# The scale of a norm moved behind the product: H turned unscaled within the mixer's last tiles, 1/rms multiplied in at each up tile

## The reference

```python
for layer in range(DEPTH_2):
    h = _rmsnorm_2(x, norm_mix[layer])
    ...
    x = x + y
    h = _rmsnorm_2(x, norm_ffn[layer])
    x = x + _conv_ffn(h, ffn_w_up[layer], ffn_conv_w[layer], ffn_conv_b[layer], ffn_w_down[layer])

def _conv_ffn(h, w_up, conv_w, conv_b, w_down):
    S = h.shape[1]
    u = h @ w_up                      # 1024 -> 2 * 2816
    u_pad = jnp.pad(u, ((0, 0), (FFN_CONV - 1, 0), (0, 0)))
    y = conv_b.astype(u.dtype)
    for j in range(FFN_CONV):         # 3 taps along the tokens
        y = y + u_pad[:, j:j + S, :] * conv_w[j]
    gate, up = jnp.split(y, 2, axis=-1)
    return (jax.nn.silu(gate) * up) @ w_down
```

## Time and profile before

| | |
|---|---|
| median of 3 executions | 1595.07 us (1594.04 to 1595.58) |
| the profiled execution | 1594.28 us |
| its span, first to last instruction | 1592.6 us |
| mean granted TensorE clock | 0.944 of full speed |
| busy share PE, PEld, DVE, ACT | 90%, 76%, 52%, 43% |
| first mixer's last addition to H starts | 1075.24 us |
| second mixer's last addition to H starts | 1392.68 us |
| last addition of the second feed forward starts | 1587.86 us |

### The profile page before, as it was taken

The page is one execution under the profiler, slowest core; times in us unless marked ns, Lnnn a source line. Parts: engine busy times, 40 slices in busy tenths (PEclk is TensorE's granted clock), DMA queues, the critical chain, the costliest instruction groups (busy, mean ns, idle before and its releaser), DMA issues.

```text
span 1592.6 us, 27418 instructions
## 1 busy us (share of the span) xinstructions
PE 1437.8 (90%) x11661; PEld 1214.2 (76%) x11661; DVE 830.7 (52%) x1471; ACT 683.9 (43%) x1184; POOL 10.6 (1%) x10
## 2 busy tenths in 40 slices
PE   7999999999899777877777779999999998999998
PEld 6999899899865344334443679988999895899997
DVE  6775453565512111112112569667777776567775
ACT  6443544543522111111111685455555564465553
POOL 1000000000000000000000100000000000000000
PEclk9999999999989998898987999989999996999999
DMA  6454354577999999999999444233655541336553
GB/s 232 159 159 155 110 165 130 167 270 276 358 402 419 420 419 417 420 421 419 421 420 415 154 134 139 83 115 102 204 189 186 175 136 53 99 114 212 172 180 125
DMA packets 173711, 372.03 MB, mean 234 GB/s; under 512 B 6912, under 2 KB 141184, under 8 KB 149008
## 3 DMA queue, kind: packets, MB, share of 16 engines
q1 hardware_dynamic: 173584, 370.21, 63.0%
HBM read 369.14 MB, written 1.05 MB: 232 GB/s over the span
## 4 chain that ended last, share of the span: by engine, by line
PE 65%; DMA 22%; DVE 6%; ACT 5%; issue 1%; SPq 1%; DVEq 0%; ACTq 0%
PE bank L581 17%; PE bank L582 16%; PE bank L583 16%; DMA wu<-in_expert_w_up_dram 14%; DMA wu<-in_expert_w_down_dram 5%; PE bank L1625 3%; PE bank L737 3%; DMA raw<-in_hgrn_w_in_dram 2%; DVE lo L545 2%; PE bank L1597 2%; ACT hi L534 1%; PE bank L1663 1%; PE bank L871 1%; DMA raw<-in_w_in_dram 1%; PE bank L846 1%
## 5 line engine op out<-in xcount | busy, mean ns | idle before, releaser
L545 DVE TENSOR_TENSOR lo<-raw,hi 128x1024 fp32r<-128x1024 f32 (+2 forms) x315 | 371.9, 1215 | 214.3 <-ACT hi L534 213.4
L581 PE MATMUL bank<-XH,hi 128*128 128x256 f32 x1416 | 406.8, 287 | 4.3 <-DVE lo L545 2.2
L582 PE MATMUL bank<-XL,hi 128*128 128x256 f32 x1416 | 401.8, 284 | 0.0
L583 PE MATMUL bank<-XH,lo 128*128 128x256 f32 x1416 | 401.5, 284 | 0.0
L534 ACT ACTIVATE hi<-raw 128x1024 fp32r<-128x1024 f32 (+2 forms) x315 | 317.2, 1047 | 74.5 <-PE bank L583 18.3
L581 PEld LDWEIGHTS bank<-XH,hi 128*128 128x128 f32 x1416 | 272.9, 193 | 12.3 <-issue 6.6
L582 PEld LDWEIGHTS bank<-XL,hi 128*128 128x128 f32 x1416 | 272.6, 193 | 0.8
L583 PEld LDWEIGHTS bank<-XH,lo 128*128 128x128 f32 x1416 | 272.4, 192 | 0.0
L1625 PE MATMUL bank<-wu,xg 128*32 128x256 f32 x2048 | 172.7, 439 | 52.0 <-DMA wu<-in_expert_w_up_dram 48.1
L1625 PEld LDWEIGHTS bank<-wu,xg 128*32 128x32 f32 x2048 | 71.8, 122 | 128.2 <-DMA wu<-in_expert_w_up_dram 66.3
L1663 PE MATMUL bank<-wu,hidT 128*32 128x256 f32 x1024 | 75.6, 412 | 35.4 <-DMA wu<-in_expert_w_down_dram 29.9
(11 more groups left out here) (347 smaller groups left out, 2203.2 us busy)
## 6 DMA issues: line engine op xcount, KB each, us to landing
wu<-in_expert_w_gate_dram SPq DMA_DIRECT2D x64, 1024.0 KB, 27.1
wu<-in_expert_w_up_dram SPq DMA_DIRECT2D x64, 1024.0 KB, 26.8
wu<-in_expert_w_down_dram SPq DMA_DIRECT2D x64, 1024.0 KB, 27.3
raw<-in_w_in_dram SPq DMA_DIRECT2D x44, 1024.0 KB, 5.2
raw<-in_ffn_w_up_dram SPq DMA_DIRECT2D x44, 1024.0 KB, 5.2
raw<-in_ffn_w_down_dram SPq DMA_DIRECT2D x22, 1024.0 KB, 5.0
raw<-in_hgrn_w_in_dram SPq DMA_DIRECT2D x16, 1024.0 KB, 5.4
raw<-in_w_branch_ret_dram SPq DMA_DIRECT2D x8, 1024.0 KB, 6.9
```

What stands on the lines that cost most here:

```text
L545: dve.tensor_tensor(lo_of(u), v, hi_of(u), ALU.subtract).then_inc(*WL.inc(u))
L581: pe.matmul(dst, first[0], first[1], start=start, stop=False)
L582: pe.matmul(dst, second[0], second[1], start=False, stop=False)
L583: return pe.matmul(dst, third[0], third[1], start=False, stop=stop)
```

## The change

- H is turned unscaled. `pe_turns` is a side of the mixer's last four tiles: after the first token half of tiles 1, 2 and 3 TensorE turns quarter 0, 1 and 2 of H (`pe_piece`, 4 transposes, into banks 4 to 6). ScalarE and VectorE make XH and XL of it with the gain alone (`act_piece`, `dve_piece`), and the squares of each quarter (`act_piece_squares`, `dve_piece_squares`).
- The first gate tile (`first`) goes to two banks, one a unit: K steps 0 to 5 of unit 0, the turn of quarter 3, K steps 0 to 5 of unit 1, the row of 1/rms (`pe_rows`: two matmuls of ones with a diagonal of 1/rms, so that each partition has the row), then K steps 6 and 7 of both units.
- VectorE copies the row to `rsb` and multiplies each up or gate tile by it, from the bank to `us` in SBUF (`scaled`); all taps read `us`. The bank is free after that multiplication.
- The splits in the feed forward are placed anew. ScalarE: up to u + 7 before the g taps, u + 8 between taps and silu, u + 9 before the up taps. VectorE: up to u + 6 before the g multiplication, u + 7 behind it, u + 8 before the up multiplication, u + 9 behind it, ahead of the taps. None stands behind DL but after the last group. The sides take one step a tile, not two.
- The Sqrt table is loaded in the mixer's first output tile, not behind its last.

```diff
     m = Room(region, tr_at)
-    xsF = m.new([P, 2, D], F32)
...
+    us, rsb, diag = [m.new([P, 2, T], F32) for _ in range(2)], m.new([P, T], F32), m.new([P, 2, P], F32)
+    sq_a, sq_d = m.new([P, 4, 256], F32), m.new([P, 4, 256], F32)
...
+        def pe_piece(i, p, made):
...
+            pe.wait_ge(*made.got("H", p))
+            for j in range(2):
+                for t in range(2):
+                    k = 2 * p + j
+                    done = pe.transpose(b.ap[:, j * T + t * P:j * T + t * P + P], H[:, t, k * P:(k + 1) * P], ident)
...
+        def pe_turns(i, made):
+
+            yield
+            for p in range(3):
+                yield
+                pe_piece(i, p, made)
+                yield
+
+        def pe_rows(i):
...
+            for t in range(2):
+                pe.wait_ge(*NORM.dve.got(i, "diag", t))
+                done = pe.matmul(b.ap[:, t * P:(t + 1) * P], C("ones"), diag[:, t, :], start=True, stop=True)
...
+        def dve_scale(i):
+            dve.wait_ge(*NORM.act.got(i, "sq", 3))
+            dve.wait_ge(*NORM.dve.got(i, "sq", 3))
+            dve.tensor_reduce(st[:, 48:50], st[:, 40:48].rearrange("p (t n) -> p t n", t=2), AX.X, ALU.add).then_inc(*NORM.dve.inc(i, "sums"))
+            dve.wait_ge(*NORM.act.got(i, "root"))
+            dve.reciprocal(st[:, 52:54], st[:, 50:52]).then_inc(*NORM.dve.inc(i, "rstd"))
+            dve.wait_ge(*NORM.dve.got(i, "rstd"))
+            for t in range(2):
+                dve.tensor_scalar(diag[:, t, :], ident, st[:, 52 + t:53 + t], None, ALU.mult).then_inc(*NORM.dve.inc(i, "diag", t))
...
+        def act_result(n, unit, made, w0):
+            for i in range(4):
+                act_wide(unit(i), AHEAD)
+                if i == 0:
+                    act_warm(ACT.Sqrt)
+                else:
+                    act_piece_squares(n, i - 1, made)
+                    act_piece(n, i - 1, "norm_ffn_2", w0)
+            act_piece_squares(n, 3, made)
+            act_root(n)
+            act_piece(n, 3, "norm_ffn_2", w0)
+
+        def dve_result(n, unit, made, w0):
+            for i in range(4):
+                dve_wide(unit(i), AHEAD)
+                if i:
+                    dve_piece(n, i - 1, "norm_ffn_2", w0)
+                dve.wait_ge(*WU.got(unit(i) + 1))
+                hs = H[:, :, 256 * i:256 * i + 256]
+                dve.tensor_tensor(hs, hs, b_[i].rearrange("p (t n) -> p t n", t=2), ALU.add).then_inc(*made.inc("H", i))
+                dve_piece_squares(n, i, made)
+            dve_scale(n)
+            dve_piece(n, 3, "norm_ffn_2", w0)
+            dve_rows(n)
...
+                for part in (range(6), range(6, 8)):
+                    for j in range(2):
...
+                        if k == 7:
+                            done.then_inc(*WU.inc(u + j))
+                        elif j == 0:
+                            pe_piece(4 + 2 * l, 3, made)
+                        else:
+                            pe_rows(4 + 2 * l)
...
+                dve.tensor_tensor(us[name == "u"][:, :, :], b_[(2 * j + (name == "u")) % 4].rearrange("p (h n) -> p h n", h=2),
+                                  rsb[:, :].rearrange("p (h n) -> p h n", h=1).to_broadcast([P, 2, T]), ALU.mult).then_inc(*F.dve.inc("us", name, j))
...
             for j in range(FT // 2):
                 r = j % 2
-                dve_tile(unit2(ffn_tile(l, "g", j)), 2, AHEAD, sides)
+                u = unit2(ffn_tile(l, "g", j))
+                dve_split(u + 7)
+                step(*sides)
+                scaled("g", j)
+                dve_split(u + 8)
                 other_taps("g", j, Y[0][r], 2 * j)
-                dve_tile(unit2(ffn_tile(l, "u", j)), 2, AHEAD, sides)
+                dve_split(u + 9)
+                step(*sides)
+                scaled("u", j)
+                dve_split(u + 10)
                 other_taps("u", j, Y[1][r], FT + 2 * j)
...
-                if j:
-                    dve_split(unit2(ffn_tile(l, "d", j - 1)) + 2 + AHEAD)
```

More of the change, by code:

```diff
@@ new lines, in pe_turns @@
+        def pe_turns(i, made):
[5 more added lines that the diff above has]
+        def pe_rows(i):
+            b = bank[4]
+            for s, key in b.taken:
+                pe.wait_ge(*s.got(*key))
+            for t in range(2):
+                pe.wait_ge(*NORM.dve.got(i, "diag", t))
+                done = pe.matmul(b.ap[:, t * P:(t + 1) * P], C("ones"), diag[:, t, :], start=True, stop=True)
+            done.then_inc(*NORM.pe.inc(i, "rows"))
+            b.taken = [(NORM.dve, (i, "rsb"))]
@@ new lines, in act_root, with dve_piece_squares @@
+        def act_root(i):
+            act.wait_ge(*NORM.dve.got(i, "sums"))
+            act.activation(st[:, 50:52], st[:, 48:50], ACT.Sqrt, bias=epst[:, 0:1], scale=1.0 / D).then_inc(*NORM.act.inc(i, "root"))
+        def dve_piece_squares(i, p, made):
+            dve.wait_ge(*made.got("H", p))
+            dve.scalar_tensor_tensor(sq_d[:, p, :], H[:, 1, 256 * p:256 * p + 256], 1.0, H[:, 1, 256 * p:256 * p + 256], ALU.mult,
+                                     ALU.mult, accum_out=st[:, 44 + p:45 + p]).then_inc(*NORM.dve.inc(i, "sq", p))
@@ L2123, in act_hgrn @@
                 step(*sides)
-            for i in range(4):
-                act_wide(unit2(16 + i), AHEAD)
-            act_warm(ACT.Sqrt)
+            act_result(4, lambda i: unit2(16 + i), HG.dve, 0)
         def dve_hgrn():
@@ L2184, in ffn_tile, with pe_ffn, first @@
             return t + n
-        def pe_ffn(l, sides):
+        def pe_ffn(l, made):
             F, x = FF[l], normed(4 + 2 * l)
-            pe_norm(4 + 2 * l, xsF)
+            def first():
+                u = unit2(ffn_tile(l, "g", 0))
+                for b in (bank[0], bank[2]):
+                    for s, key in b.taken:
+                        pe.wait_ge(*s.got(*key))
+                    b.taken = [(F.dve, ("us", "g", 0))]
+                for part in (range(6), range(6, 8)):
+                    for j in range(2):
+                        pe.wait_ge(*WH.got(u + j))
+                        pe.wait_ge(*WL.got(u + j))
+                        for k in part:
+                            for s, key in x(k):
+                                pe.wait_ge(*s.got(*key))
+                            done = three(b_[2 * j][:, 0:T], hi_of(u + j)[:, k, :], lo_of(u + j)[:, k, :], XH[:, k, :], XL[:, k, :],
+                                         False, k == 0, k == 7)
+                        if k == 7:
[4 more added lines that the diff above has]
+                            pe_rows(4 + 2 * l)
             def down(j, final):
@@ L2541, in act_mla @@
                     attend(h - 4)
-            for i in range(4):
-                act_wide(unit2(O_TILE + i), AHEAD)
-            act_warm(ACT.Sqrt)
+            act_result(6, lambda i: unit2(O_TILE + i), ML.dve, 8)
         def dve_mla(after):
@@ L2682, in dve_mla @@
                     attend(h - 4)
-            for i in range(4):
-                dve_wide(unit2(O_TILE + i), AHEAD)
-                dve.wait_ge(*WU.got(unit2(O_TILE + i) + 1))
-                hs = H[:, :, 256 * i:256 * i + 256]
-                dve.tensor_tensor(hs, hs, b_[i].rearrange("p (t n) -> p t n", t=2), ALU.add).then_inc(*X.dve.inc("H", i))
+            dve_result(6, lambda i: unit2(O_TILE + i), ML.dve, 8)
         rest_ = {}
```

96 lines of the change are left out of this document (63 added, 33 removed).

## The result

The changed kernel took 1581.03 us (median of 4 runs, 1577.41 to 1583.74), the kernel before, timed beside it, 1594.55 us (4 runs, 1592.74 to 1595.58): ratio 0.9915, 95% interval 0.9888 to 0.9942, a gain of 13.5 us. The profiled execution took 1583.74 us, span 1582.4.

A forecast was written before the change was run, and what follows sets the result against it. TensorE bounds the feed forward, with the norm ahead of it a hole. Terms -11.2 - 1.0 + 1.3 + 0.9 = -10.0 us gave a median of 1585.0 us, range 1581.0 to 1591.5.

The forecast's parts named there:

- going between kinds of matmul: At the two edges, TensorE changing kind of matmul ten times in all, 0.08 us each: 0.8 us of cost.
- lateness at the end of the first feed forward: Lateness of the group's chain not made good before the first feed forward's last down tile: +0.9 us.
- Part 1: Two edges: H's last addition to the first gate tile's end falls from 13.7 to 6.4 us; sum -11.2 us.
- Part 2: First feed forward: the weight-split wait at group 2's up tile goes, -1.0 us.
- Part 3: Every up or gate tile: 22 multiplications of 0.69 us per feed forward, covered as busy time; taps counted as unchanged.
- Part 4: Last down tile of each feed forward: DL late by 0.8 us in the first, 0.5 in the second; +1.3 us.
- Part 5: Group chain: starts some 5 us late, recovers 0.55 to 0.95 us a group, leaves +0.9 us in the first feed forward.
- the deepest case of the sum: Whole kernel: the largest gain claimed for any case, -13.5 us.
- A: Rival at the edges: they close only partly, XL or the diagonal late; gain 4 to 8 us, about 1589; chance 0.12.
- D: Rival at the edges: norm not shortened, the mixer's last tiles grow by what the edge loses; chance 0.01.
- C: Rival: no lateness at the end, nothing for changing kinds; -12 to -13.5 us, about 1582; chance 0.07.
- B: Rival in the feed forwards: chain longer than TensorE's group; no change (1594.5) to +6.6 us (1601.7); chance 0.14.

The follow-up runs named there:

- the shorter end: Changed kernel with the multiplication in halves, each with its own wait, and the last group's split moved behind DL: 1580.5 us (0.9919), again 1582.94 us (0.9947).

## Why the prediction was right or wrong

I predicted 1585.0 us, a gain of 10.0; by its stages the change is worth 11.4, and the first timing gave 13.5, outside the 8 to 12 that I called the forecast. Its 1581.03 us lie at the very bottom of my range. The mechanism was right, the sum too small. What failed is the size of two terms: the 0.8 us for going between kinds of matmul, which measured about nothing, and the 0.9 us of lateness at the end of the first feed forward, which measured nothing.

*Part 1, the edges: right, but for one term.* The first tile's end at 6.4 behind the last addition: TensorE starts its next tile at 6.37 and 6.43, busy all the way, at full clock. Two slips cancel in this: TensorE starts the tile 0.2 us ahead of the addition, and the rows of 1/rms (L732) are four records, not two, 0.43 us instead of 0.32. The 12 transposes at 1.3: 1.35 and 1.24. Cover of XL and of the diagonal: no wait on either. The 13.7 was 0.2 too long, since it ended with ScalarE's start and the 6.4 with TensorE's tile. Measured alike, the two edges save 7.09 + 7.06 = 14.15 and the tiles and the stage between give back 2.65, so 11.5, where I had 12.0. **The term that failed is the 0.8 for going between kinds of matmul**: the transposes run doubled and single leave between nothing and 0.07 us for six changes. I had taken it from a slow transpose of the earlier trace rows, which stands behind a hole, at lowered clock, and so could not price this.

*Part 2, the order of the splits: the size right, the weight wrong.* The wait of 1.1 went, as priced. But I treated this as a small item beside the multiplication. It is what the multiplication rests on: with the old order, the changed kernel is 56 us slower, and the new order alone changes nothing that can be measured. "As busy time it costs nothing: the matmuls cover it" was true only because of part 2, and nothing in my working said so. I summed VectorE's busy time of a group and never walked the two engines through their written order with the multiplication in it and the splits left where they were.

*Part 3, the multiplication:* 21 at 688 ns a feed forward and two halves, as priced. The taps from SBUF: VectorE's 480 ns against 477 from the bank, ScalarE's two 1.09 to 1.10 against 1.02. By the Trainium skill's VectorE: DVE Perf Modes (The TRN2 errata) the taps of one tile, two on ScalarE and four on VectorE, would have become, by an estimate, some 0.2 us shorter, which the rows do not show: of its two directions ScalarE's agrees with the rows and VectorE's does not.

*Part 4, the ends:* 0.8 and 0.5 forecast, 0.8 and 0.5 in the waits, both on DL. The attribution held too: the run without multiplications kept the 0.8 and lost the 0.5.

*Part 5, lateness: wrong by its whole 0.9.* Recovery was as worked out or a little better: from group 4 on late groups take 16.0 to 16.1 us of chain (I had 16.0 to 16.4) against 16.98, so nearly 1 us a group. What I had too large was the start. Counted back from DL of the last group in steps of 16.99, DL was 4.1 us late in group 1, where I had 5.2. The angles added the 2.5 that I had: DL came 18.01, 16.22 and 16.54 us after the one before in groups 2 to 4, against 16.37, 16.00 and 15.84 in the second feed forward, which has no angles. That makes 6.6 in all, not 7.7, and a part was made good meanwhile, so that the most was 5.1, in group 2. The lateness was gone by group 8, with the wait at the end the same 0.8 that the kernel before shows with the new order alone.

Summed: edges -11.5 (forecast -12.0), kinds of matmul 0 (+0.8), order -1.1 (-1.0), ends +1.3 (+1.3), lateness 0 (+0.9), unexplained -0.1: -11.4 (-10.0). That the unexplained is so small is in part luck: it is -0.2 in FF 0 and +0.1 in FF 1. Without the two allowances for things that no row showed, 1.7 together, the forecast would have been -11.7. Each was taken from within a bound whose lower end was zero, and in both zero was right, or nearly. The further 2.1 us of the first timing are not in the stages that the change touches, and the two later timings did not show them.

The range had a fault of its own: its lower end, 1581.0, was 0.6 us below the deepest case of the sum (1595.07 - 13.5 = 1581.6), with next to nothing for the scatter of a median. The kernel before alone had medians from 1592.5 to 1595.1 us, and three timings of the change gave 9.4, 13.5 and 11.6 us.

Of the rivals, A and D did not occur. C was right in its reasons (no lateness, nothing for changing kinds) and too deep in its sum. B did not occur here, but it is real: half a microsecond more of chain (multiplication twice at the up tile) already leaves lateness that costs 6.5 us, and with the old order the chain is longer than TensorE's group, 18.58 us.

## What to carry to other kernels

A norm's scale can be applied behind the product, and then only the matmul operands stand ahead of the first tile; here that made the way to the second tile 7.1 us shorter, twice, for 1.3 us of transposes each time and 0.7 us for the multiplications. When two in-order engines hand work to and fro, a new step costs what its place makes of it: put other ready work between the two halves of a hand-over, walk both engines through their written order, and compare the cycle with the bound engine's own, since below that a longer chain costs only the lateness that it fails to make good, and above it costs every group. A cost that no row shows and that is bounded from zero needs both ends in the range, and the range needs the scatter of the measurement beside them.

## What the runs showed of the hardware that I had not expected

**The stretch of lowered clock behind one and the same hole differs in length.** The 2.70 us from 6.5 us behind the last addition on, at both edges of the kernel before:

```profile
1081.74:1084.44 2.70, 2.70 (x15) 2.70 (x14) 2.63 (x7) 2.69 (x6) 0.00 (x0) 0.52 0.00 0
1399.18:1401.88 2.70, 2.70 (x15) 2.70 (x14) 2.63 (x7) 2.69 (x6) 0.00 (x0) 0.52 0.00 0
```

The same in the kernel before with the new order:

```profile
1083.76:1086.46 2.70, 2.70 (x23) 2.70 (x22) 2.63 (x6) 2.69 (x5) 0.00 (x0) 0.91 0.00 0
1400.18:1402.88 2.70, 2.70 (x19) 2.70 (x19) 2.70 (x6) 2.59 (x4) 0.00 (x0) 0.72 0.00 0
```

The hole is the same (3.3 us of waiting), the matmuls in the 2.70 us behind it are 15 and 15, 23 and 19. At 2.70 x (0.91 - 0.52) = 1.05 us this is most of that run's 1.65 us, and at 2.70 x (0.72 - 0.52) = 0.54 of its 0.91; with the 0.3 of the waits in FF 0 that leaves 0.3 and 0.4 unexplained. So the one trace of the kernel before had long stretches at both edges, and had it had those of the kernel with the new order, the change would have been worth some 1.6 us less by its stages, an estimate (1.05 + 0.54). The norm of the attention, which the change left alone, shows it between versions too: 0.77 in the changed kernel, 0.55 with the shorter end. What decides it I did not try to find. An edge with a hole scattered by about 1 us in these traces; the edges without one show no such scatter, as FF 0 and FF 1 of the changed kernel repeat within 0.02 us over three traces.

**Transposes of 128 columns between matmuls of 256 cost 0.10 to 0.1125 us each**, with no fixed part that shows and no loss of clock, even 12 in a row behind the last tile.

**The attention stage differs in length from trace to trace, with unchanged code.** Less the transposes, it took between 118.1 and 121.7 us in these traces. One wait in it is 4.8 us in two traces of the changed kernel, 4.2 in the third, and 3.9 with the shorter end. It does not simply go with the end of the feed forward ahead: with the multiplication twice at the gate tiles the feed forwards are as long as in the changed kernel, and the wait is 4.0. I did not follow this further.
